# Conformer depthwise convolution on TensorE: all taps as stacks of four shifted copies on four column tiles, the copies made by DMA, and layer norm by running sums

## What is computed

```
def conformer_conv(h, w_pw1, b_pw1, w_dw, b_dw, ln_g, ln_b, w_pw2, b_pw2):
    a, gate = jnp.split(h @ w_pw1 + b_pw1, 2, axis=-1)
    u = a * jax.nn.sigmoid(gate)
    dw = lax.conv_general_dilated(
        u, w_dw[:, None, :], window_strides=(1,), padding=((CONV_WIDTH - 1, 0),),
        dimension_numbers=('NWC', 'WIO', 'NWC'), feature_group_count=D_MODEL) + b_dw
    d32 = dw.astype(jnp.float32)
    mu = jnp.mean(d32, axis=-1, keepdims=True)
    var = jnp.mean(jnp.square(d32 - mu), axis=-1, keepdims=True)
    z = (d32 - mu) * lax.rsqrt(var + EPS) * ln_g + ln_b
    z = jax.nn.silu(z).astype(h.dtype)
    return z @ w_pw2 + b_pw2
```

## Time and profile before

| | |
|---|---|
| time, median of 3 runs | 1181.57 us (1181.31 to 1181.78) |
| the profiled execution | 1181.89 us, its span 1180.1 us |
| granted TensorE clock, mean | 0.989 |
| PE busy | 1154.5 us, 98% |
| DVE busy | 879.3 us, 75% |
| ACT busy | 638.6 us, 54% |
| moved by DMA | 197.66 MB, mean 167 GB/s |

### The profile page before, as it was taken

How to read it: one execution, slowest core, us unless ns; L and a number is a source line. 1 busy time by engine, 2 the same in 40 slices (tenths; PEclk the granted TensorE clock), 3 DMA queues, 4 the chain that set the end, 5 groups by cost and what they waited for, 6 DMA issues and landing times.

```text
span 1180.1 us, 18431 instructions
## 1 busy us (share of the span) xinstructions
PE 1154.5 (98%) x7116; PEld 1031.4 (87%) x7116; DVE 879.3 (75%) x1422; ACT 638.6 (54%) x1053; POOL 30.8 (3%) x54
## 2 busy tenths in 40 slices
PE   8999999999999799999999999999999889999998
PEld 8998888888999698888889998888888668888887
DVE  6868877765899578777666867877765897877753
ACT  6645555544746366656543545656544566665641
POOL 0110000000000000000000000000001200000000
PEclk8999999999999799999999999999999999999999
DMA  7633555565322055555653655555553323555552
GB/s 283 228 124 127 183 200 189 179 215 179 108 96 83 5 194 180 194 179 187 205 179 143 215 179 179 182 197 193 202 190 143 143 73 114 194 194 179 189 207 68
DMA packets 29033, 197.66 MB, mean 167 GB/s; under 512 B 3473, under 2 KB 4753, under 8 KB 5521
## 3 DMA queue, kind: packets, MB, share of 16 engines
q1 hardware_dynamic: 28656, 196.34, 47.7%
q10 hardware_dynamic: 288, 0.14, 0.1%
HBM read 195.41 MB, written 1.05 MB: 166 GB/s over the span
## 4 chain that ended last, share of the span: by engine, by line
PE 96%; DVE 2%; ACT 1%; DMA 1%; issue 0%; POOL 0%; SPq 0%; DVEq 0%; ACTq 0%
PE banks L381 41%; PE banks L387 21%; PE banks L359 7%; PE banks L420 7%; PE banks L362 7%; PE banks L365 7%; PE banks L403 1%; PE banks L409 1%; PE banks L406 1%; DMA raw_t<-w 1%; PE banks L1335 0%; DVE scr L1552 0%; POOL scr L959 0%; DVE lo_t L290 0%; ACT scr L1049 0%
## 5 line engine op out<-in xcount | busy, mean ns | idle before, releaser
L290 DVE TENSOR_TENSOR lo_t<-raw_t,hi_t 128x1024 fp32r<-128x1024 f32 x368 | 444.4, 1220 | 8.6 <-ACT hi_t L284 7.2
L284 ACT ACTIVATE hi_t<-raw_t 128x1024 fp32r<-128x1024 f32 x368 | 380.4, 1050 | 55.3 <-PE banks L387 23.9
L381 PE MATMUL banks<-x,hi_t 128*128 128x512 f32 x1408 | 356.6, 393 | 0.0
L381 PEld LDWEIGHTS banks<-x,hi_t 128*128 128x128 f32 x1408 | 252.3, 189 | 44.3
L387 PEld LDWEIGHTS banks<-x,lo_t 128*128 128x128 f32 x1408 | 194.2, 190 | 15.2
L387 PE MATMUL banks<-x,lo_t 128*128 128x256 f32 x1408 | 198.8, 282 | 0.0
L381 PE MATMUL banks<-f,hi_t 128*128 128x512 f32 x704 | 181.2, 392 | 0.0
L381 PEld LDWEIGHTS banks<-f,hi_t 128*128 128x128 f32 x704 | 124.8, 189 | 20.6
L359 PE MATMUL banks<-x,hi_t 128*128 128x256 f32 x448 | 130.5, 291 | 2.6 <-ACT hi_t L284 2.6
L365 PE MATMUL banks<-x,lo_t 128*128 128x256 f32 x448 | 128.0, 286 | 0.5 <-DVE lo_t L290 0.5
L362 PE MATMUL banks<-x,hi_t 128*128 128x256 f32 x448 | 127.8, 285 | 0.0
(11 more groups left out here) (171 smaller groups left out, 1201.9 us busy)
## 6 DMA issues: line engine op xcount, KB each, us to landing
raw_t<-w SPq DMA_DIRECT2D x183, 1024.0 KB, 4.9
raw_t<-w SPq DMA_DIRECT2D x2, 512.0 KB, 7.7
out<-h SPq DMA_DIRECT2D x8, 128.0 KB, 3.8
cst<-consts SPq DMA_DIRECT2D x1, 800.0 KB, 11.7
h<-xT SPq DMA_DIRECT2D x1, 768.0 KB, 8.0
h<-xT SPq DMA_DIRECT2D x1, 256.0 KB, 4.4
pw<-poolw SPq DMA_DIRECT2D x1, 256.0 KB, 13.7
col<-cols SPq DMA_DIRECT2D x1, 193.0 KB, 8.7
```

The source lines that it names most:

```text
L284: e.activation(hi_t[:, p % RING, :], raw_of(p), ACT.Copy).then_inc(s_hi, 1)
L290: e.tensor_tensor(lo_t[:, p % RING, :], raw_of(p), hi_t[:, p % RING, :].bitcast(F32), ALU.subtract).then_inc(s_lo, 1)
L381: e.matmul(halves(banks[:, to[j], :]), hi_t[:, slot, r * P:(r + 1) * P], parts[:, ks[j], :, :], start=ks[j] == 0, stop=False, skip_group_c ...
```

## The change

The PW1 product uses `broad_run` instead of `tile`; ACT first copies half of the banks (into `cb`), DVE adds and then scales. All 32 taps (31 and a zero) are done on PE. For each block, the gated input is written to a DRAM tensor `shifts` and read back as a stack: a row of `stack` along the free axis holds the four groups of 32 channels one after the other, and the 128 partitions hold each group's 32 channels four times, shifted by 0 to 3 positions. A matmul with 128 rows then covers four taps of 32 channels; its 32 output columns are one of four column tiles, and eight steps m (shifted by 4m) cover 32 taps. The weights of a block are eight times four matrices of 128 x 32, built by one DVE operation from a mask and the tap columns (`diagonals`). The tap chains on DVE, the diagonals on ACT and the channel means of each block go. Layer norm subtracts a partial mean of the first two blocks (`shift`) on the way out of the bank, keeps running sums of values and squares, and applies factor and mean by two spread banks. In `broad_run` the waits for activations stand before each k. The FFN's last k are one run.

```
             for c in range(RAW, w.shape[0]):
                 load_chunk(e, c)
+                if 0 <= c - G_PW1 // 16 - 5 < KD:
+                    load_stack(e, c - G_PW1 // 16 - 5)
...
                 e.wait_ge(s_hi, at)
-            if arrives:
-                e.wait_ge(*arrives[0])
-                e.wait_ge(*arrives[1])
             for j in range(n):
                 slot, r = piece(e, g + j)
+                if arrives and (j == 0 or ks[j] != ks[j - 1]):
+                    e.wait_ge(*arrives(ks[j])[0])
+                    e.wait_ge(*arrives(ks[j])[1])
...
                     g = g0 + UP_TILES + KF * n + k
                     to = min(KF, k + 8 - g % 8)
-                    if n == 0 and to == KF:
-                        to = max(k, KF - 2) if k < KF - 2 else k + 1
-                    broad_run(e, g, [bank] * (to - k), range(k, to), f2, KF - 1, f_of(s, to - 1) if n == 0 else None)
+                    broad_run(e, g, [bank] * (to - k), range(k, to), f2, KF - 1,
+                              (lambda k: f_of(s, k)) if n == 0 else None)
                     k = to
...
+        US_C, NU = 288, 3
+        u_r = [scratch(n * US_C, US_C) for n in range(NU)]
...
+        NS = 3
+        stack = [scratch(C3 + n * 4 * US_C, 4 * US_C) for n in range(NS)]
+        C4 = C3 + NS * 4 * US_C
+        diags = [scratch(C4 + n * PIECE, PIECE).rearrange("p (a b c) -> p a b c", a=4, b=8) for n in range(NS)]
+        assert C4 + NS * PIECE <= SCR
...
+        CPAIRS = (0, 6, 4)
+        CONV_BANKS, STAT_BANK, NORM_BANKS = (3, 2), 6, (7, 0)
...
+        def load_stack(e, u):
+            e.wait_ge(s_cu, u + 1)
+            by_row = bass.AP(shifts, u * 32 * 4 * US_C, [[US_C, 4], [4 * US_C, 32], [1, US_C]])
+            e.dma_start(by_row, u_r[u % NU]).then_inc(s_kept, 16)
+            if u >= NS:
+                e.wait_ge(s_conv, u - NS + 1)
+            e.wait_ge(s_kept, 16 * (u + 1))
+            again = bass.AP(shifts, u * 32 * 4 * US_C, [[1, 4], [4 * US_C, 32], [1, 4 * US_C - 3]])
+            e.dma_start(stack[u % NS][:, 0:4 * US_C - 3], again).then_inc(s_stack[u % NS], 16)
         def pe_conformer(e):
             for u in range(KD):
-                if u >= len(UP_BANKS):
-                    e.wait_ge(s_cup, u - len(UP_BANKS) + 1)
+                if u >= len(CPAIRS):
+                    e.wait_ge(s_cup, u - len(CPAIRS) + 1)
+                if u == 1:
+                    pe_col_sums(e, 2)
+                if u == 2:
+                    pe_spread(e, 2)
                 for t in range(2):
...
+                    broad_run(e, G_PW1 + 16 * u + 8 * t, [CPAIRS[u % 3] + t] * KD, range(KD), x2, KD - 1,
+                              (lambda k: x_of(2, k)) if u == 0 and t == 0 else None)
+                if u == 3:
+                    pe_conv(e, 0)
+                    pe_conv(e, 1)
+                if u == 5:
+                    e.wait_ge(s_dw, 2)
+                    plain(e, banks[:, CONV_BANKS[1], 0:T], one[:, :], dw[:, 0, :], True, False)
+                    plain(e, banks[:, CONV_BANKS[1], 0:T], one[:, :], dw[:, 1, :], False, True).then_inc(s_cpart, 1)
+                    pe_conv(e, 2)
+                    e.wait_ge(s_shift, 1)
+                    pe_conv(e, 3)
+            for u in range(4, KD):
+                pe_conv(e, u)
+            ps = banks[:, STAT_BANK, :]
+            e.wait_ge(s_sums, 2)
+            pe_stat(e, ps[:, 0:2], sum_d, True, False)
+            pe_stat(e, ps[:, 2:4], sum_q, False, False)
+            e.wait_ge(s_dw, KD)
+            pe_stat(e, ps[:, 0:2], dw[:, 7, :], False, True)
+            e.wait_ge(s_csq, 7)
+            pe_stat(e, ps[:, 2:4], dsq[:, 7 % NQ, :], False, True).then_inc(s_cstat, 1)
+            for n in range(2):
+                e.wait_ge(s_cdg, n + 1)
+                plain(e, banks[:, NORM_BANKS[n], 0:T], one[:, :],
+                      dg4[:, 2 * n:2 * n + 2, :].rearrange("p a b -> p (a b)")).then_inc(s_csp, 1)
             pe_out_blocks(e, 2, G_PW2, N_CONF, range(KD), 0, 8 * N_CONF)
             pe_out_rest(e, 2, G_PW2, N_CONF, range(KD))
...
+        def pe_conv(e, u):
+            e.wait_ge(s_diag, u + 1)
+            e.wait_ge(s_stack[u % NS], 16 * (u // NS + 1))
             if u >= 2:
                 e.wait_ge(s_dw, u - 1)
...
+            for m in range(8):
+                for g in range(4):
+                    out_g = banks[32 * g:32 * g + 32, CONV_BANKS[u % 2], 0:T]
+                    last = plain(e, out_g, diags[u % NS][:, g, m, :], stack[u % NS][:, g * US_C + 4 * m:g * US_C + 4 * m + T], m == 0, m == 7)
+            last.then_inc(s_conv, 1)
...
-                e.wait_ge(s_cup, u + 1)
+                e.wait_ge(s_tiles, upto(c - 1))
+                if u:
+                    e.wait_ge(s_cup, u)
+                e.activation(halves(cb), c_pair(u, 1), ACT.Copy).then_inc(s_cside, 1)
+                hi_to(e, c + 3)
+                for v in ((), (0, 1))[u == 1] if u < 2 else (u,):
+                    e.wait_ge(s_cscaled, v + 1)
+                    if v >= 2:
+                        e.wait_ge(s_cu, v - 1)
+                    e.activation(cs_r[v % 2], ct_r[v % 2][:, T:2 * T], ACT.Sigmoid,
+                                 bias=colv("b_pw1", 8 + v)).then_inc(s_sig, 1)
...
+            e.activation(cs_r[0][:, 0:1], cs_r[0][:, 0:1], ACT.Silu)
...
+            def add(u):
+                e.wait_ge(s_cside, u + 1)
                 if u >= 2:
                     e.wait_ge(s_cu, u - 1)
...
+                e.tensor_tensor(halves(ct_r[u % 2]), c_pair(u, 0), halves(cb), ALU.add).then_inc(s_cup, 1)
...
+            def glu(u):
+                e.wait_ge(s_cpad, 1)
+                e.wait_ge(s_sig, u + 1)
+                e.wait_ge(s_cscaled, u + 1)
+                if u >= NU:
+                    e.wait_ge(s_kept, 16 * (u - NU + 1))
+                e.scalar_tensor_tensor(u_r[u % NU][:, 30:30 + T], ct_r[u % 2][:, 0:T], colv("b_pw1", u), cs_r[u % 2],
+                                       ALU.add, ALU.mult).then_inc(s_cu, 1)
...
+                    e.wait_ge(s_conv, u - NS + 1)
+                by_tap = col[:, COLS["w_dw"] + 32 * u:COLS["w_dw"] + 32 * u + 32]
+                e.tensor_tensor(diags[u % NS].rearrange("p a b c -> p (a b) c"), stretch(mask, 1, 32), stretch(by_tap, 2, 32),
+                                ALU.mult).then_inc(s_diag, 1)
+            def take(u):
+                ps = banks[:, CONV_BANKS[u % 2], 0:T]
+                e.wait_ge(s_conv, u + 1)
+                if u < 2:
+                    e.tensor_scalar(dw[:, u, :], ps, colv("b_dw", u), None, ALU.add).then_inc(s_dw, 1)
+                else:
+                    e.scalar_tensor_tensor(dw[:, u, :], ps, colv("b_dw", u), shift, ALU.add, ALU.subtract).then_inc(s_dw, 1)
...
+            lo_to(e, G_PW1 + 16)
             dve_mean(e, 2)
+            add(0)
             dve_dg(e, 2)
-            lo_to(e, G_PW1 + 20)
+            diagonals(0)
+            lo_to(e, G_PW1 + 32)
+            add(1)
             dve_rbc(e, 2)
-            for u in range(KD):
-                c = G_PW1 + max(16 * (u + 1), 20)
+            scale(0)
+            scale(1)
+            diagonals(1)
+            glu(0)
+            glu(1)
+            for u in range(2, KD):
+                c = G_PW1 + 16 * (u + 1)
                 lo_to(e, c)
...
+                add(u)
+                scale(u)
+                lo_to(e, c + 3)
+                glu(u)
+                if u not in (5, 7):
+                    diagonals(u)
+                if u == 3:
+                    take(0)
+                    take(1)
+                if u == 5:
+                    e.wait_ge(s_cpart, 1)
+                    e.tensor_scalar(shift, banks[:, CONV_BANKS[1], 0:T], 1.0 / (2 * P), None, ALU.mult).then_inc(s_shift, 1)
+                    e.wait_ge(s_shift, 1)
+                    e.tensor_tensor(dw[:, 0:2, :], dw[:, 0:2, :], stretch(shift, 1, 2), ALU.subtract).then_inc(s_cen, 1)
+                    lo_to(e, c + 11)
+                    e.wait_ge(s_cen, 1)
+                    e.tensor_tensor(sum_d, dw[:, 0, :], dw[:, 1, :], ALU.add).then_inc(s_run, 1)
+                    e.wait_ge(s_csq, 1)
+                    e.tensor_tensor(sum_q, dsq[:, 0, :], dsq[:, 1, :], ALU.add).then_inc(s_run, 1)
+                    take(2)
+                    diagonals(5)
+                    take(3)
+                    for v in (2, 3):
+                        e.wait_ge(s_run, 2 * (v - 1))
+                        gather(v, v)
             lo_to(e, G_PW2)
...
+            for u in range(4, KD - 1):
+                take(u)
+                if u == 4:
+                    diagonals(7)
+                e.wait_ge(s_run, 2 * (u - 1))
+                gather(u, u, u == KD - 2)
+            take(KD - 1)
+            ps = banks[:, STAT_BANK, :]
+            e.wait_ge(s_cstat, 1)
+            n = dv.mark(e.tensor_scalar(st[:, 2:4, :], ps[:, 0:4].rearrange("p (a b) -> p a b", a=2), 1.0 / D, None, ALU.mult))
...
```

(51 more changed lines are left out.)

197 lines of the change are left out of this document (64 added, 133 removed).

## The result

The changed kernel takes 1229.84 us (median of 4 runs, 1227.76 to 1229.90) against 1181.44 us (4 runs, 1180.23 to 1181.78): ratio 1.0407, 95% interval 1.0389 to 1.0425, some 48 us slower where 17 us faster were forecast. The profiled execution took 1229.8 us, its span is 1227.9.

The account below looks back on a forecast made before the run. TensorE, busy 98% of the span, was taken as the bound. Stage 89.0 + 0.6 + 3.4 = 93.0 us instead of 112.0, -19.0; FFN +1.2: 1181.9 - 17.8 = 1164 us, range 1156 to 1181.

Parts of the forecast that it names:

- A block of this queue thus costs 1.5 + 1.9 + 3.4 + 0.5 = 7.3 us: SP's queue in the conformer stage: fixed part, stack read, weight chunk and gated-input write add to 7.3 us a block.
- 1.5 us fixed and 3.35 us a 1024 KB: DMA rate taken from 128 KB in 1.9 us and 1024 KB in 4.9 us, used for chunk, write and stack.
- the DMA chain is the bound: Stack reads: 3.8 us gives 1175, 8 us some 20 slower; 18% for 1171 to 1179, 5% for slower than before.
- Column tiles: Convolution taps on PE: four column tiles run at once, 0.44 us a step, 3.53 us a block, 28.2 us in all.
- Both rivals with slower tiles: Convolution taps: two at once, 0.88 us a step, 1182 us, 5%; no overlap, 1.77 us a step, 1238 us, 6%.
- The floor: Conformer stage with no late stack and no gap: PW2 at 82.5 us, time 1154 to 1157 us.
- The closing chain: From the last taps to PW2, the layer norm, silu and split: 7.2 us against 12.8.
- PW1 in runs: PW1 matmuls in runs of eight tiles, 2.79 us a run: 44.7 instead of 46.1 us, a gain of 1.4.
- the eighth k: Start of PW1: its operands are wanted 0.65 us before they exist, adding 0.65 us.
- The clock: PE's waits of 2.8 and 3.6 us for stacks each bring a half-clock loss of 1.7 us, 3.4 together.
- FFN tails: FFN's last two k no longer set apart: the last operand's matmul waits 0.3 us, four times, +1.2 us.
- Small transfers slip past the chunk: Rival for SP's queue: no stack is late, PW2 at 82.5 us, time 1154 to 1157 us; 6%.

Follow-up runs that it names:

- Without copies: The changed kernel with the stack writes and reads left out, stacks zeroed once by POOL and all matmuls kept: 1153.82 us.
- both orders joined: The changed kernel with sixteen-engine copies, SP's queue as in "another order" up to block 4, then no chunk ahead of writes 5 and 7: 1158.42 us.
- another order: The changed kernel with sixteen-engine copies, one write and four reads a block, SP's queue reordered so blocks 0 and 1 precede a weight chunk: 1167.40 us.
- the version with sixteen engines: The changed kernel with each copy cut into four transfers of outer dimension 32, same bytes, queue and order: 1172.64 us.
- two engines: The changed kernel with each copy cut into two transfers of outer dimension 2: 1276.04 us.

## Why the prediction was wrong

**The step that failed** is "A block of this queue thus costs 1.5 + 1.9 + 3.4 + 0.5 = 7.3 us", and in it the rate of "1.5 us fixed and 3.35 us a 1024 KB" for stack and write. That rate is of transfers of 128 rows; a chunk keeps nearly all sixteen engines busy (share 0.92 at 381 GB/s in 306 to 308 of the changed kernel). I carried it over by bytes and did not look at the outer dimension, which the diff shows. The terms measured: stack 8 us for 1.9, write 1.9 for 0.5, chunk 2.8 for 3.4, fixed 3.7 for 1.5, cycle 16.4 for 7.3. Of the 9.1 us that were missing, 7.5 are the rate and 2.2 the fixed part; the chunk gives back 0.6. PE has 9.3 us of work a block, so at 16.4 the DMA chain was the bound.

**The rival "the DMA chain is the bound"** was the right one, with 5% for slower than before. Its own pricing was wrong too: at a stack of 8 us it gave 20 us slower, and 48 came. By the prediction's terms its cycle would be 1.5 + 8 + 3.4 + 0.5 = 13.4 us; from the first read to the last it was 16.3 on average, seven times 2.9, 20 of the missing 28 us. It left the write at 0.5 and the fixed part at 1.5. The last block at the lower clock (6.2 us for 3.5) is another 2.7; the rest I can't place. Its criterion ("a stack that lands over 5 us after its issue with nothing before it") is what the last read shows.

**Column tiles: right.** Four at once: 0.438 us a step against 0.44, 3.66 us a block against 3.53 (a block alone shows its last latency). Both rivals with slower tiles are out, and no cost of imperfect overlap appeared. The Trainium skill (TensorE: Matmul & The Clock Gate, "Measured speedup vs the span model") has 3.07 for four row tiles; the estimate from it was 36.8 us for the eight blocks. Without copies the eight took 7.11 + 7.11 + 14.02 = 28.2 us.

**The floor: right.** Without a late stack the prediction had PW2 at 82.5 + 0.6 us into the stage and 1154 to 1157 us. Without copies it is 83.5 us (293.38 to 376.90), and 1153.82.

**The closing chain:** 7.2 predicted, 7.7 measured (369.19 to 376.90), 12.8 before. **PW1 in runs:** 2.79 us a run of eight, as taken; the eighth k was 0.52 us late (L381 behind DVE x L315), for 0.65. **DVE** is no longer full, as said. Its 57.4 of 159 us in the changed kernel are diluted by the waits; without copies it is busy 59.7 of 83.8 us, 71%, where it was 93.8 of 112.0.

**The clock:** the sign was right for the long waits, and the price low: 1.7 us taken, 1.8 to 2.8 lost in each block that followed a wait of 7.5 to 11.2 us. Most of such a block is slow, not all of it (0.50 in 438.3 to 442, 0.80 in 443 to 444.4). For waits of the size that was predicted (2.8 and 3.6 us) the price doesn't always hold. In "both orders joined" the block behind a wait of 2.83 us took 3.66 us, at a granted clock of 1.00 in the wait and after it; in "another order" 4.5 us of wait cost 1.7.

**FFN tails:** +1.2 predicted, +1.6 measured with an interval of 0.6 to 2.7. The last operand is 0.23 us late (0.9 us over four), 0.3 predicted.

**"Small transfers slip past the chunk"** did not happen. In the version with sixteen engines the writes issued from 315.88 on, behind a stack and a chunk, were awaited until 323.47.

**What stays open:** why two engines carry more than half of four's rate; how much of the 1.6 us of the tails is more than their 0.9 us of waits; what the rest of 3.7 us in the cycle is made of; and how the place in the queue and POOL's own issue share in the versions where a write was late. The 4.6 us between the best version and the one without copies (1158.42, 1153.82) are hardly open: the stage is 4.0 us longer in the profiled executions (87.5 and 83.5), and the waits for stacks are 4.2.
